# Hybrid trunk on one core: at the head of the input stage, token tiles two and three become loads of their own ahead of the first weights, and the turns, copies and low parts stand in another order

## The reference, cut to what matters

```python
meta = jnp.broadcast_to(meta_tokens.astype(x.dtype)[None], (b, N_META, D_MODEL))
h = jnp.concatenate([meta, x], axis=1)
...
# rms_norm(h, gdn_norm_g): h * rsqrt(mean(h*h) + EPS) * gain
# gdn_mixer(...), first line:
proj = h @ w_in          # w_in: 1024 x (4*1024 + 16)
```

## Time and profile before

| | |
|---|---|
| median of 3 runs | 2775.98 us (2775.92 to 2777.08) |
| the profiled execution | 2779.09 us, span of its instructions 2777.0 us |
| PE busy | 2723.8 us (98%), 19450 instructions |
| PE weight loads | 2494.9 us (90%) |
| DVE, ACT, POOL busy | 1992.2 us (72%), 1071.6 us (39%), 1216.6 us (44%) |
| DMA | 298.40 MB, mean 107 GB/s |

### The profile page before, as it was taken

The page is one execution under the profiler, slowest core; times in us unless marked ns, Lnnn a source line. Parts: engine busy times, 40 slices in busy tenths (PEclk is TensorE's granted clock), DMA queues, the critical chain, the costliest instruction groups (busy, mean ns, idle before and its releaser), DMA issues. The chain is left out here.

```text
span 2777.0 us, 48746 instructions
## 1 busy us (share of the span) xinstructions
PE 2723.8 (98%) x19450; PEld 2494.9 (90%) x19450; DVE 1992.2 (72%) x2504; ACT 1071.6 (39%) x1994; POOL 1216.6 (44%) x1054
## 2 busy tenths in 40 slices
PE   8999999999999999999999999999999999999998
PEld 7999998888999999999999998788887888888887
DVE  5777536887469777778778444577747988888888
ACT  5222224554443322333434201477744333334434
POOL 3000015556245656566564100233223666666775
PEclk9999998999999999999999999999999999999999
DMA  4333333222202232334431425555320323325432
GB/s 126 92 93 85 92 124 102 94 96 79 81 24 89 100 115 85 104 111 170 169 127 46 154 100 155 162 121 122 93 61 20 103 100 104 103 99 205 167 128 97
DMA packets 215995, 298.40 MB, mean 107 GB/s; under 512 B 9915, under 2 KB 151372, under 8 KB 215772
## 3 DMA queue, kind: packets, MB, share of 16 engines
q1 hardware_dynamic: 205194, 257.01, 29.5%
q0 software_dynamic: 10368, 38.21, 4.0%
q10 hardware_dynamic: 210, 0.07, 0.0%
HBM read 212.08 MB, written 83.19 MB: 106 GB/s over the span
## 5 line engine op out<-in xcount | busy, mean ns | idle before, releaser
L2137 DVE TENSOR_TENSOR RL<-RAW,RH 128x512 fp32r<-128x512 f32 (+1 forms) x408 | 412.9, 1014 | 185.0 <-ACT RH L1516 183.1
L1516 ACT ACTIVATE RH<-RAW 128x512 fp32r<-128x512 f32 (+1 forms) x408 | 248.0, 617 | 652.1 <-PE PS L2852 220.3
L2849 PE MATMUL PS<-QP,RH 128*128 128x512 f32 x1584 | 487.7, 389 | 0.0
L2852 PE MATMUL PS<-QP,RH 128*128 128x260 f32 x1584 | 414.2, 283 | 0.0
L2851 PE MATMUL PS<-QP,RH 128*128 128x260 f32 x1584 | 414.0, 283 | 0.0
L2849 PEld LDWEIGHTS PS<-QP,RH 128*128 128x128 f32 x1584 | 297.4, 188 | 62.0 <-issue 0.2
L2849 PE MATMUL PS<-QP,RL 128*128 128x512 f32 x792 | 309.1, 390 | 2.9 <-DVE QP L2154 1.6
L2851 PEld LDWEIGHTS PS<-QP,RH 128*128 128x128 f32 x1584 | 299.6, 189 | 0.0
L2852 PEld LDWEIGHTS PS<-QP,RH 128*128 128x128 f32 x1584 | 299.0, 189 | 0.0
L1146 POOL TENSOR_TENSOR RAW<-RAW 128x512 f32<-128x512 f32 (+1 forms) x136 | 205.6, 1512 | 174.3 <-DVE RL L2137 169.0
L2414 PE MATMUL PS<-YH,WL 128*128 128x348 f32 (+1 forms) x744 | 241.7, 325 | 2.3 <-DVE WL L1769 2.3
(11 more groups left out here) (376 smaller groups left out, 6965.8 us busy)
## 6 DMA issues: line engine op xcount, KB each, us to landing
RAW<-in_ffn_w_gate_up SPq DMA_DIRECT2D x44, 1024.0 KB, 5.2
s_in<-obuf POOLq DMA_DIRECT2D x32, 520.0 KB, 4.4
raw<-in_gdn_w_in SPq DMA_DIRECT2D x32, 512.0 KB, 4.1
RAW<-in_ffn_w_down SPq DMA_DIRECT2D x16, 1024.0 KB, 5.4
QF<-s_a SPq DMA_DIRECT2D x12, 1040.0 KB, 8.4
QF<-s_a SPq DMA_DIRECT2D x12, 1024.0 KB, 7.7
s_a<-ua SPq DMA_DIRECT2D x22, 520.0 KB, 2.8
s_a<-ua SPq DMA_DIRECT2D x22, 512.0 KB, 3.3
```

The costliest lines, as they stand in the source:

```text
L1516: act.activation(m.RH[n % m.ring][:, 0:kn, :], m.weight_block(p, i), ACT.Copy).then_inc(m.f_hi[0], 1)
L2137: dve.tensor_tensor(m.RL[n % m.ring][:, 0:kn, :], m.weight_block(p, i), m.RH[n % m.ring][:, 0:kn, :].bitcast(F32), ALU.subtract).then_inc( ...
L2849: done = pe.matmul(acc, w, x, start=first, stop=last)
L2852: done = pe.matmul(acc[:, 1, :], w, x[:, 1, :], start=first, stop=last)
```

## The change

The change reorders the head of the input stage; no instruction's shape is changed.

- SP: the load of tiles 2 and 3 is cut into two loads, both ahead of weights 0. Loads of tiles 4 to 6 and of 7 and 8 keep their places; the latter counts on the first group's semaphore.
- PE: turn 2 stands ahead of the transpositions of the parameters; chunk (0,0) stands ahead of turn 5 (before: behind it), chunk (1,0) ahead of turn 7 (before: behind it).
- DVE: the parameter copies come behind the copy of tile 2 (before: tile 1), and the gain of weights 0 directly behind them; the low part of weights 0 stands ahead of the low part of tile 3. The low part of tile 1 goes to POOL.
- POOL makes the low parts of tiles 1, 2, 4, 6, 8 (before: 2, 4, 6, 8), and `Y_NEED` counts accordingly.

```diff
-        X_GROUP = [0, 0, 1, 1, 2, 2, 2, 3, 3]
-        ON_POOL = (2, 4, 6, 8)
+        X_GROUP = [0, 0, 1, 2, 3, 3, 3, 0, 0]
+        ON_POOL = (1, 2, 4, 6, 8)
         OPENED = {(0, 0): 1, (1, 0): 2, (0, 1): 3, (1, 1): 4, (0, 2): 5, (1, 2): 6}
-        Y_NEED = [(3, 1), (4, 3), (5, 4)]
+        Y_NEED = [(2, 2), (3, 4), (4, 5)]
...
             sp.dma_start(xin[:, 0:1, :], xv[:, 0:1]).then_inc(x_in[0], 16)
+            sp.dma_start(xin[:, 1:2, :], xv[:, 1:2]).then_inc(x_in[1], 16)
+            sp.dma_start(xin[:, 2:3, :], xv[:, 2:3]).then_inc(x_in[2], 16)
             in_weight(0)
-            sp.dma_start(xin[:, 1:3, :], xv[:, 1:3]).then_inc(x_in[1], 16)
             sp.wait_ge(x_in[0], 32)
-            sp.dma_start(xin[:, 3:6, :], xv[:, 3:6]).then_inc(x_in[2], 16)
+            sp.dma_start(xin[:, 3:6, :], xv[:, 3:6]).then_inc(x_in[3], 16)
             in_weight(1)
-            sp.dma_start(xin[:, 6:8, :], xv[:, 6:8]).then_inc(x_in[3], 16)
+            sp.dma_start(xin[:, 6:8, :], xv[:, 6:8]).then_inc(x_in[0], 16)
...
-                act.wait_ge(x_tr, 2 * i + (1 if i < 2 else 3))
+                act.wait_ge(x_tr, 2 * i + (1 if i < 3 else 3))
...
-                dve.wait_ge(x_tr, 2 * i + (2 if i < 2 else 4))
+                dve.wait_ge(x_tr, 2 * i + (2 if i < 3 else 4))
...
-                if i == 1:
-                    dve.wait_ge(x_tr, 6)
+                if i == 2:
+                    dve.wait_ge(x_tr, 8)
                     dve.tensor_copy(pvec[:, 0:121], PS[:, 0, 0:121]).then_inc(p_cp, 1)
...
-                if i == 2:
                     gain(0, GN, 16)
+                if i == 3:
+                    lo(0, 1)
                 if i not in ON_POOL:
                     low(i)
-                if i == 3:
-                    lo(0, 1)
...
-                if i in (0, 2, 4, 7):
-                    pe.wait_ge(x_in[X_GROUP[i]], 32 if i == 0 else 16)
+                if i in (0, 2, 3, 4, 7):
+                    pe.wait_ge(x_in[X_GROUP[i]], 32 if i == 0 else 48 if i == 7 else 16)
...
             turn_in(1)
+            turn_in(2)
             pe.wait_ge(p_in, 16 * 7)
...
-            turn_in(2)
             turn_in(3)
             turn_in(4)
+            first_chunk(0, 0)
             turn_in(5)
-            first_chunk(0, 0)
             turn_in(6)
+            first_chunk(1, 0)
             turn_in(7)
-            first_chunk(1, 0)
             turn_in(8)
```

## The result

| | before | after |
|---|---|---|
| median of 7 runs each | 2775.5 us (2774.45 to 2777.08) | 2784.26 us (2780.01 to 2787.97) |
| ratio | | 1.0029 (95% interval 1.0020 to 1.0039) |
| the profiled execution, its span | 2779.09, 2777.0 | 2784.26, 2782.0 |
| PE busy | 2723.8 us | 2722.9 us |

The account below looks back on a forecast made before the run. PE bounds the kernel, its head setting the end: -0.4 start of chunk (0,0), +3.7 lost cover, +1.4 clock, +2.4 turn 7 and tile 8's copy give +7.1, so 2775.98 + 7.1 = 2783.1 us; range 2779.8 to 2784.8.

Parts of the forecast that it names:

- The start of chunk (0,0): Head of PE: the first chunk starts at 18.6 instead of 18.97, worth -0.4 us.
- The row of subtractions: DVE and POOL ahead of chunk (0,0): five operations on two SBUF operands take turns, the last ending at 18.55.
- Rival (a): DVE and POOL subtractions do not take turns; chunk (0,0) starts at 15.8, +4.3 us, 2780.3; chance 0.11.
- The lost cover: Ahead of chunk (1,0): turn 5's chain to weights 1's low part no longer runs under chunk (0,0); PE idles, +3.7 us.
- Turn 7: Behind chunk (1,0): turn 7 and the copy of tile 8 now come ahead of the squares, +2.4 us.
- Rival (c): Loads of tiles 2 and 3 come no earlier, landing at 10.3; chunk (0,0) at 19.2, +7.7 us, 2783.7; chance 0.08.
- The clock: Chunk (1,0): after 3.7 us of idle PE its first matmuls run at the slow level, +1.4 us.
- rival (b): PE keeps the fast level in both chunks; first spread at 50.1, +4.1 us, 2780.1; chance 0.09.
- At the length of before the chunk ends at 24.0: Chunk (0,0) on PE, started at 18.6, keeps its earlier length of 5.35 us.
- whatever moves the first spread moves the end by as much: PE behind the head: only 0.5 us of idle in 366 to absorb a shift, so the end moves equally.

Follow-up runs that it names:

- e5: The changed kernel with turn 5 alone put back ahead of chunk (0,0); 2778.99 us, ratio 1.0010.
- e2: The kernel before with only turn 5 moved behind chunk (0,0) and turn 7 behind chunk (1,0); 2784.13 us, ratio 1.0032.
- e6: The changed kernel with turn 7 alone put back ahead of chunk (1,0); 2783.02 us, ratio 1.0027.
- e7: The kernel before with the loads alone changed, tiles 2 and 3 each by itself ahead of weights 0; 2776.29 us, ratio 0.9998.
- e3: The changed kernel with 29 unread transpositions on PE ahead of chunk (1,0); 2786.73 us, ratio 1.0041.
- e8: The changed kernel with the low parts of tiles 1 and 2 on DVE instead of POOL; one execution, 2783.94 us.
- e9: e7 with tile 2's low part on DVE too and weights 0's low part ahead of tile 3's; 2775.61 us, ratio 0.9998.
- e1: The changed kernel with turn 5 back ahead of chunk (0,0) and turn 7 back ahead of chunk (1,0); 2776.59 us, ratio 1.0003.
- e4: The changed kernel with unread transpositions on PE, 15 ahead of chunk (0,0) and 29 ahead of chunk (1,0); 2782.03 us, ratio 1.0025.

## Why the prediction was right, point by point

The steps of the sum, with the measured ones beside them:

| step | predicted | after |
|---|---|---|
| start of chunk (0,0) | 18.6 | 18.65 |
| length of chunk (0,0) | 5.35 | 6.03 |
| from its end to the start of chunk (1,0) | 5.3 | 5.36 |
| length of chunk (1,0) | 5.35 | 5.47 |
| from its end to the first spread | 18.4 | 18.51 |
| first spread | 53.05 | 54.02 |
| against before's 45.99 | +7.06 | +8.03 |

**The start of chunk (0,0)** came as reckoned, and for the reason given. The row of subtractions was put down as gain to 14.1, POOL's second to 16.35, low part of weights to 17.45, low part of tile 3 to 18.55; the rows above end at 14.10, 16.33, 17.41 and 18.55. Rival (a), no taking of turns, falls by the same rows. That the order of the first two doesn't matter was shown by chance: in e5 DVE's gain came first. Timelines of DVE and POOL in e5:

```profile
10.72 1.22 DVE L1775 TENSOR_TENSOR raw<-raw,pvec 128x1024 f32<-128x1024 f32 x1
...
13.07 2.19 DVE L1770 TENSOR_TENSOR WL<-raw,WH 128x1024 fp32r<-128x1024 f32 x1 [0.51 <-ACT WH L1249]
15.18 3.37 DVE L1782 TENSOR_TENSOR YL<-hT,YH 128x1024 fp32r<-128x1024 f32 x1
```

```profile
10.77 6.70 POOL L997 TENSOR_TENSOR YL<-hT,YH 128x1024 fp32r<-128x1024 f32 x2
```

There the gain is short and the last low part long, and chunk (0,0) starts at 18.66. The Trainium skill ("SBUF — State Buffer", Who interferes with whom) has it that whichever of the two engines issues first holds the ports they share for its whole instruction while the other stands still; both traces agree, the loser's length being 3.31, 2.19 or 3.37 us instead of 1.2.

**The lost cover**, 3.7 predicted and 5.36 - 1.66 = 3.70 measured, was e2's 3.45 us of idle PE in a kernel that has no other change. **Turn 7** was right too: +2.4 predicted, 18.51 - 16.10 = 2.41 measured, and e6 shows it by taking it back. Rival (c), loads that come no earlier, falls by e7; in after the turns 0 to 2 end at 5.14 + 4.61 = 9.75, and the gain starts at 10.79, where the sum had 9.8 and 10.9.

**The clock** is where the sum was too small. That both chunks would hold slow matmuls was right, so rival (b) falls, but not all of it came the way the prediction had it: in after the level had fallen before turn 4 already, in the wait for tile 4's load, and not in the wait ahead of the chunk, which was 3.50 us (2.8 predicted) because turn 4 started at 13.19 and not at 14.09. Chunk (0,0) was taken at before's length of 5.35 and took 6.03. This is the step "At the length of before the chunk ends at 24.0", a term mis-sized by 0.68 of the 0.97 by which the whole is off; chunk (1,0) gives 0.12, and the remaining 0.2 lies in the other three. In before, after and the eight experiments without filling ahead of it this chunk begins slow; its length in them runs from 5.20 (e3) to 6.65 (e8), with no order that the kernels explain: 5.24 in e2, 5.42 in e9, 5.52 in e7, 6.62 in e1. In chunk (1,0), after the 3.45 us gap, it was 5.47 in after and in e8, and 6.62 in e2. So the term should have been 1.3 to 2.7 us for each of the two chunks, not a fixed 1.44 for the first and nothing to 3.05 for the second. The Trainium skill ("TensorE: Matmul & The Clock Gate", What's actually happening) says that the number of slow matmuls at the start of one kernel varies from run to run, 6, 11 or 14 of them. The prediction named this and worked 0.8 to 1.8 us out of it; that it varies agrees with these traces, and the 2.7 us that were lost in e1, e2 and e8 are more than that range.

**The time.** +7.1 was predicted, +8.0 is the ratio's, +8.03 the head's. The measured 2784.26 lies 0.5 us below the upper end of the range, and that it lies inside is in part luck: with both chunks as slow as in e1 and e2 (6.62) the same sum would have been 9.6 instead of 7.1, and upward the range had nothing for chunk (0,0) or for the stretch behind the first projection. The claim that whatever moves the first spread moves the end by as much held on the ratios: e2 +8.78 in the head and 0.32%, 8.9 us, in time; e6 +5.3 and 0.27%, 7.5 us, with 5.3 in its interval; e5 +1.5 and 0.10%, 2.8 us; e1 +0.94 and 0.03%; e4 +5.0 and 0.25%, 6.9 us, with 5.0 in its interval. It did not hold on single profiles (the profiled execution was set at 2786.2 and took 2784.26, for the stretch at 420 to 440 of before), nor on e3's ratio, where it takes runs of equal granted clock.

## What to carry to other kernels

An instruction that is moved forward on the bottleneck engine takes the place of the one it passes, and with it all that hung on that one: here a turn of 0.83 us was what started a 5.4 us chain over DVE and ACT, and the chunk ahead of it was the cover for that chain. Before moving such a step, follow what it displaces to its last consumer over every engine's queue, and count from the new start; the gain at the front (0.3 us at chunk (0,0) in after, 1.3 at the first spread in e9) is to be set against that. Keeping the bottleneck engine busy in the new gap gives back the clock (1.5 us) but not the wait (3.7 us), and an earlier first chunk is worth nothing if the second one then waits.

## What the runs showed of the hardware

- The stretch behind the first projection is at a granted clock of 0.57 in before's execution (420 to 440), 0.83 in after's (428 to 448) and 0.57 in e3's (425.5 to 445.5). The same operations took 2.7 us longer in before's than in after's, a third of the effect under study, and no edit here touches them. A mark inside the trace (the first spread, 54.02 and 51.27) separated after from e6 where the intervals of the times, some 3 us on each side, overlap.
- 24 equal matmuls took 3.9 us at the fast level and 5.2 to 6.65 us where they began at the slow one. The length did not follow the length of the wait ahead of them: 5.24 after 3.33 us (e2), 6.62 after 3.32 us (e1).
- The column of the granted clock read 1.00 over the head of e7 while its matmuls stood 0.29 us apart, as at 0.50 elsewhere; where a trace begins, the spacing decides.
- 29 transpositions whose result nobody reads, 3.33 us of them in a wait, kept PE at the fast level (e3: 3.93 us for the next 24 matmuls, 5.47 in after), and chunk (1,0) started no earlier for it behind the end of chunk (0,0) (5.36 in both).
- Where DVE and POOL worked on two SBUF operands beside each other, the order of the first two decided which instruction was long, not when the last one ended: 18.55 in after with POOL first, 15.18 + 3.37 = 18.55 in e5 with DVE first.
